# Another order of the 24 matmuls of a weight panel, in three stages of a one-core decoder layer

## The reference

```python
xn = _rmsnorm(h, norm1_g[l])
proj = xn @ w_in[l]                 # q, k, v, conv inputs, gated-attention inputs, three gate groups
ya = fox_attention(...) @ w_a_o[l]
yb = (sc_b * _causal_dwconv(sc_c * sc_h, conv_w[l])) @ w_b_o[l]
yc = (jax.nn.silu(rc) * oc) @ w_c_o[l]
mix = sigmoid(g_a + ..) * ya + sigmoid(g_b + ..) * yb + sigmoid(g_c + ..) * yc
h = h + mix @ w_o[l]
u = _causal_dwconv(_rmsnorm(h, norm2_g[l]) @ w_up[l], mlp_conv_w[l])
u_gate, u_up = jnp.split(u, 2, axis=-1)
h = h + (jax.nn.silu(u_gate) * u_up) @ w_down[l]
return _rmsnorm(h, final_norm_g)[:, N_META:]
```

## Time and profile before

| | |
|---|---|
| time of three runs | 1746.2, 1746.72 and 1748.32 us, median 1746.72 us |
| span of the profiled execution, first to last instruction | 1745.1 us |
| TensorE matmul busy | 1734.3 us (99%), 13429 instructions |
| TensorE weight loads busy | 1680.7 us (96%), 13429 instructions |
| VectorE, ScalarE, GpSimd busy | 1117.8, 763.7, 263.3 us |
| DMA | 320.62 MB, mean 184 GB/s |
| mean granted TensorE clock | 0.999 of 2.4 GHz |

### The profile page before, as it was taken

How to read it: one execution, slowest core, us unless ns; L and a number is a source line. 1 busy time by engine, 2 the same in 40 slices (tenths; PEclk the granted TensorE clock), 3 DMA queues, 4 the chain that set the end, 5 groups by cost and what they waited for, 6 DMA issues and landing times.

```text
span 1745.1 us, 34098 instructions
## 1 busy us (share of the span) xinstructions
PE 1734.3 (99%) x13429; PEld 1680.7 (96%) x13429; DVE 1117.8 (64%) x1607; ACT 763.7 (44%) x921; POOL 263.3 (15%) x494
## 2 busy tenths in 40 slices
PE   9999999999999999999999999999999999999998
PEld 8999999999999999999999999999999999888886
DVE  6857766667565554555556687777777777554454
ACT  6635444354354444444444444334444444343433
POOL 3153332630530000000000043321000000000000
PEclk9999999999999999999999999999999999999999
DMA  8567557666565655556645566666555565665654
GB/s 232 169 180 186 168 149 198 176 175 178 153 184 181 189 178 178 175 182 194 201 159 192 181 195 192 204 200 192 183 182 181 180 186 180 223 190 189 189 192 134
DMA packets 310296, 320.62 MB, mean 184 GB/s; under 512 B 17353, under 2 KB 285133, under 8 KB 310093
## 3 DMA queue, kind: packets, MB, share of 16 engines
q1 hardware_dynamic: 296861, 311.01, 58.2%
q0 software_dynamic: 12928, 7.80, 2.0%
q10 hardware_dynamic: 432, 0.79, 0.1%
HBM read 311.10 MB, written 2.11 MB: 179 GB/s over the span
## 4 chain that ended last, share of the span: by engine, by line
PE 99%; DVE 0%; DMA 0%; ACT 0%; SPq 0%; issue 0%; ACTq 0%; DVEq 0%
PE ps L1435 27%; PE ps L1437 27%; PE ps L1436 27%; PE ps L1693 5%; PE ps L1692 5%; PE ps L1691 5%; PE ps L1526 0%; DMA xb<-in_x_dram 0%; PE ps L1540 0%; PE ps L1565 0%; PE ps L1555 0%; PE ps L1556 0%; PE ps L1584 0%; PE ps L1585 0%; DVE xl L941 0%; DVE lo L896 0%
## 5 line engine op out<-in xcount | busy, mean ns | idle before, releaser
L896 DVE TENSOR_TENSOR lo<-raw,hi 128x1024 fp32r<-128x1024 f32 x584 | 709.9, 1229 | 494.4 <-ACT hi L627 490.2
L1435 PE MATMUL ps<-xh,hi 128*128 128x260 f32 (+1 forms) x3328 | 945.8, 284 | 0.2 <-DVE xl L941 0.2
L1437 PE MATMUL ps<-xh,lo 128*128 128x260 f32 (+1 forms) x3328 | 941.7, 283 | 0.0
L1436 PE MATMUL ps<-xl,hi 128*128 128x260 f32 (+1 forms) x3328 | 936.5, 281 | 0.0
L627 ACT CAST hi<-raw 128x1024 fp32r<-128x1024 f32 x584 | 604.8, 1048 | 671.8 <-PE ps L1437 539.0
L1436 PEld LDWEIGHTS ps<-xl,hi 128*128 128x128 f32 x3328 | 626.6, 188 | 0.2
L1435 PEld LDWEIGHTS ps<-xh,hi 128*128 128x128 f32 x3328 | 625.2, 188 | 1.3 <-issue 0.4
L1437 PEld LDWEIGHTS ps<-xh,lo 128*128 128x128 f32 x3328 | 624.7, 188 | 0.0
L610 POOL DMA_DIRECT2D hT<-h2b x128 | 69.6, 553 | 604.3 <-DVE h2b L1289 599.7
L1693 PE MATMUL ps<-lo,act_h 128*128 128x512 f32 x350 | 138.5, 396 | 0.0
L1692 PE MATMUL ps<-hi,act_l 128*128 128x512 f32 x350 | 137.3, 392 | 0.0
(11 more groups left out here) (298 smaller groups left out, 1383.6 us busy)
## 6 DMA issues: line engine op xcount, KB each, us to landing
raw<-in_w_in_dram SPq DMA_DIRECT2D x224, 512.0 KB, 3.6
raw<-in_w_up_dram SPq DMA_DIRECT2D x176, 512.0 KB, 4.6
raw<-in_w_down_dram SPq DMA_DIRECT2D x88, 512.0 KB, 4.7
raw<-in_w_o_dram SPq DMA_DIRECT2D x32, 512.0 KB, 3.4
raw<-in_w_in_dram SPq DMA_DIRECT2D x32, 256.0 KB, 4.2
raw<-in_w_a_o_dram SPq DMA_DIRECT2D x16, 512.0 KB, 4.3
raw<-in_w_b_o_dram SPq DMA_DIRECT2D x16, 512.0 KB, 3.3
raw<-in_w_c_o_dram SPq DMA_DIRECT2D x16, 512.0 KB, 3.3
```

Source lines behind the costliest of these rows:

```text
L896: nc.vector.tensor_tensor(part(ph, i, q, lo_all), raw[:, s, :], part(ph, i, q, hi_all).bitcast(F32), ALU.subtract).then_inc(lo_ready, 1)
L1435: nc.tensor.matmul(acc, w_hi, mh, start=first and j == 0, stop=False)
L1436: nc.tensor.matmul(acc, w_hi, ml, start=False, stop=False)
L1437: ins = nc.tensor.matmul(acc, w_lo, mh, start=False, stop=last and j == KJ - 1)
```

## The change

`use_ordered` takes the place of `use_panel` in the stages `GT`, `WO` and `UP`. It issues the same 24 matmuls with the same operands into the same two PSUM banks, in an order given by a list of (m, j, product). The order belongs to the panel's place in its trip. `BR` and `DN` are as before. The waits ahead of the panel and the increment of `panel_used` on the last matmul are as before; the start flag stands on the first matmul of each bank in the new order, the stop flag on the last.

```diff
+            KINDS = ((hi, 0), (hi, 1), (lo, 0))
+            HIGH, LOW_X, LOW_W = range(3)
+            def by_row(*rows):
+                return [(m, j, kind) for m in range(2) for j in rows for kind in range(3)]
+            def by_kind(*rows):
+                return [(m, j, kind) for m in range(2) for kind in range(3) for j in rows]
+            def by_two(*rows):
+                passes = (((0, HIGH), (0, LOW_W)), ((0, LOW_X), (1, LOW_X)), ((1, HIGH), (1, LOW_W)))
+                return [(m, j, kind) for both in passes for j in rows for m, kind in both]
+            def by_six(*rows):
+                return [(m, j, kind) for j in rows for m in range(2) for kind in range(3)]
+            UP_ORDERS = [by_row(0, 2, 1, 3)] * 4 + [by_row(0, 3, 1, 2)] * 4
+            GT_ORDERS = [by_kind(0, 1, 2, 3)] * 4 + [by_kind(0, 2, 1, 3)] * 4 + [by_kind(0, 2, 3, 1)] * 4
+            BO_ORDERS = [by_kind(0, 3, 2, 1)] * 6
+            WO_ORDERS = [by_six(0, 1, 2, 3)] * 4 + [by_two(0, 3, 1, 2)] * 4
+            def use_ordered(ph, i, q, st, moving, n, first, last, order):
+                pe.wait_ge(lo_ready, ph.panel(i, q) + 1)
+                s = ph.slot(q)
+                for at, (m, j, kind) in enumerate(order):
+                    weights, side = KINDS[kind]
+                    own = [k for k in range(len(order)) if order[k][0] == m]
+                    ins = nc.tensor.matmul(pset(st, n)[:, m, :], tiles(weights, s, j, m), moving(j)[side],
+                                           start=first and at == own[0], stop=last and at == own[-1])
+                ins.then_inc(panel_used, 1)
...
-                    use_panel(GT, i, q, st, mv, NC, kq == 0, kq == last)
+                    use_ordered(GT, i, q, st, mv, NC, kq == 0, kq == last, (GT_ORDERS + BO_ORDERS)[q])
...
-                    use_panel(WO, i, q, st, (lambda k0: lambda j: (mix_h[:, k0 + j, C0:T], mix_l[:, k0 + j, C0:T]))(kq * KJ),
-                              NC, kq == 0, kq == 3)
+                    use_ordered(WO, i, q, st, (lambda k0: lambda j: (mix_h[:, k0 + j, C0:T], mix_l[:, k0 + j, C0:T]))(kq * KJ),
+                                NC, kq == 0, kq == 3, WO_ORDERS[q])
...
-                    use_panel(UP, i, q, st, x_window(kq * KJ, C0, NC), NC, kq == 0, kq == 3)
+                    use_ordered(UP, i, q, st, x_window(kq * KJ, C0, NC), NC, kq == 0, kq == 3, UP_ORDERS[q])
```

## The result

The changed kernel takes 1750.15 us (median of 16 runs, 1749.17 to 1751.55) against 1746.71 us (16 runs). The ratio is 1.0019, 95% interval [1.0012, 1.0026]: slower by 3.4 us, small but clear of noise, where 1742.1 us was forecast. The time lies in the stated range, on the wrong side of no change.

A forecast was written before the change was run, and what follows sets the result against it. TensorE's matmul pace, 118.9 ns, was taken as the only bound. Changed panels at 2.84 instead of 2.853 us save 0.013 x 352 = 4.6 us: span 1740.5, plus 1.6 for the median, 1742.1 us; range 1731 to 1752 us.

The forecast's parts named there:

- A switch of the PSUM bank costs nothing: WO panels: alternating banks more often adds nothing, since the one switch seen costs nothing; at 0.01 us each, 2.6 us.
- The down projection is not touched: DN, which the change leaves as before: its window stays unchanged to 0.3 us.
- this interval: Bounds for the pace of the 352 changed panels: from 19 us less to 9.3 or 11 us more.
- the panel of 2.80 us: Nearer lower bound, from UP's timeline: every row group at 0.35 us instead of a 2.853 us panel, 19 us less.
- The sum: All 352 changed panels at 2 x 1.42 = 2.84 us instead of 2.853: 4.6 us less, giving 1742.1 us.
- the part that "moves least per matmul": UP, 176 panels, half of the work: only row-group order changes, rows still in threes, 8 of 24 followers change.
- GT: that a fresh moving operand at each matmul loses nothing: GT, 144 panels: moving operand and weights tile change every matmul; loading the same tile twice before brought no saving.
- The rival "slower": Changed panels lock into starts 120.0 ns apart; all of GT, WO and UP: 9.3 us more, 1756.0 us; chance 0.20.
- the half panel behind the 272-column ones: BR: first half of a 260-column panel following 272-column panels takes 1.44 us, 120.0 ns a matmul.
- The rival's point of decision: GT and part of WO: whether changing the moving row every matmul keeps the 120.0 ns rhythm instead of letting it die out.
- its figure for GT alone: Only GT in the 120.0 ns rhythm, 3456 matmuls x 1.1 ns: 1750.5 us.
- The rival "nothing": The changed kernel's time stays within 0.2%, about 3.5 us, of no change; chance 0.27.

The follow-up runs named there:

- 0213 in single products: Changed kernel with row groups in order 0, 2, 1, 3, one product at a time, in all 352 changed panels: 1758.6 us, ratio 1.0071.
- The survey: Up projection unrolled, each of 44 four-panel groups given its own sequence or window, some leaving the computation; the 24 row orders took 2.840 to 2.900 us a panel.
- single steps: Row groups 0, 1, 2, 3 in turn, one product at a time; changed kernel with this in all 352 changed panels: 1742.18 us, ratio 0.9974.
- double steps: Moves by two row groups; in the unrolled up projection, moving rows stepping by two over fixed weights took 2.920 us a panel.
- 01233210: Row groups visited in that sequence, one product per row, in four panels of the unrolled up projection: 2.920 us a panel.
- the survey of addresses: Up projection unrolled with moving windows and weights at chosen places and widths, plus ten down-projection orders; four starts 64 bytes apart took 2.840 us a panel, 128 bytes 2.920.
- one start: Unrolled up projection with the moving window at one place for every matmul: 2.880 us a panel at columns 8, 4 and 0, 2.911 at 10.

## Why the prediction was wrong

The forecast held in these steps. TensorE is the only bound and no wait came in. The pace is what changes, in GT, WO and UP alone. It depends on what runs before a matmul (0213 in single products took 2.86, 2.88 and 2.92 us). A switch of the PSUM bank costs nothing (2.854 and 2.840 us with a switch at every matmul, against 2.853 and 2.840). The down projection is not touched (244.08 and 244.09 us from its first matmul to its last).

**The step that failed** is "The present pace lies near the upper end of this interval. That is the main argument for a direction: there is more room below than above." The lower end of that interval was the panel of 2.80 us, and further down I had put the 112 ns of the 128-column float32 matmuls, by my estimate the time of a weight load. No run shows that it is the load's time, and no order tried reached either figure; the 2.80 us was in part a rounding, since it took row groups at 0.35 us from starts rounded to 0.01 us, and the shortest of the eight row groups of an UP panel takes 352.5 ns on the mean of the kernel before, or 2.82 us a panel. The survey puts the paces of 24 orders between 2.840 and 2.900 us, and one list reached 2.920. The old one, 2.853, is the fifth best or equal to it. Below it there was 0.013 us, above it 0.067. I had measured the room to bounds that none of these orders comes near, and not to what comparable orders take. The mechanism, a pace that depends on what came before, was right; the room and with it the direction were wrong.

**The sum** took "the pace of the quicker half panel for the whole panel", 2.84 us. That pace exists, 118.3 ns a matmul, and it is what the single steps reach; with all 352 panels there the time was 1742.18 us against the 1742.1 written down. But the halves of one panel are not two rhythms to choose from: 1.42 and 1.43 us are parts of one rhythm that repeats every 24 matmuls. Whether a given list reaches 2.84 could not be read from the trace of before, and I applied it to all eight lists. Two do, in 66 of the 352 panels.

**Part by part.** UP I called the part that "moves least per matmul": its first half lost 0.27 us in all, its second 0.02 us a panel and 1.66 us in all, about half of the loss. GT: that a fresh moving operand at each matmul loses nothing was right for 0123 and nearly so for 0321, and wrong for the other two lists. **The rival "slower"** came closest: it named a lock into a slower rhythm, and GT's second and third groups run at exactly 120.0 ns. That this is the rhythm of the half panel behind the 272-column ones is not shown; in unrounded starts that half takes 1.437 us, 119.8 ns a matmul, and the half after it is back at 1.432. The rival's point of decision was wrong. A change of moving row at every matmul doesn't keep the slow rhythm going, since single steps have it too and take 118.3 ns; which sequences do is not fully explained (double steps often, 01233210 without any). That its figure for GT alone, 1750.5 us, lies 0.35 us from the measured time is luck: GT lost 1.1 us and not 3.8, and WO and UP, which that figure leaves out, lost the rest. Had it been priced for two thirds of GT's gate panels, it would have come out at 64 x 24 x 1.1 ns = 1.7 us, close to what those 64 panels cost. **The rival "nothing"**, that the order has no effect, has the size: the ratio of 1.0019 lies within its 0.2%. But the order has an effect, from 2.840 to 2.920 us a panel in the lists tried. Two results of the survey of addresses show that the moving operand alone doesn't set the pace either: half the weight columns take 0.08 us off a panel in double steps, and weight tiles moved by 32 bytes add 0.04 us in single steps. With the tiles in place, a half or a quarter of the load changes nothing in the sequence 0123 (2.840 and 2.841 us against 2.840).

## What to carry to other kernels

In this kernel, where TensorE streams the rounded parts and the remainders without a gap, the order of independent matmuls was worth up to 2.8% of their time (2.84 against 2.92 us a panel). For 260 columns from column 12 the best list found cycles through four row groups in one direction, one product at a time, with starts 64 bytes apart modulo 256. It kept 2.84 us in all of the 352 panels but five, at the start and beside small float32 matmuls. Lists that go back and forth by the same step took 2.88 and 2.92 us, and from columns 8, 4 and 0 the same list took 2.880 us, no better than one start, and with 384 columns it was worse (4.280 against 4.240), so measure it where it is to run. Such a test fits into one unrolled loop, four panels for each candidate, since settled panels repeated to the nanosecond (2.840, 2.840 and 2.840 us). Give a candidate more than one predecessor: the same list, 0213 in single products, ran at 2.86, 2.88 or 2.92 us behind another list or a break in the stream. Measure the room by what comparable orders reach, not by the pace of another form of matmul (112 ns here, where no list of 260 columns went below 118.3).

## What the runs showed of the hardware

In this stream the pace was a rhythm into which a sequence locked. Settled panels of most lists repeated to 1 ns, and most of their mean distances between starts, 118.33, 119.17, 120.0, 120.83 and 121.67 ns, lie 0.833 ns apart, or 20 ns a panel (2.840, 2.860, 2.880, 2.900 and 2.920 us); others lie between (118.6, 118.89, 119.7, 121.3 ns). One start of 260 columns repeated gave 120.0 ns, from column 10 121.3 ns. One list, 0213 in single products, ran at 119.2, 120.0 or 121.7 ns a matmul by what preceded it: another list, or small float32 matmuls that broke the stream. In the sequences tried, the loss above 118.3 ns went away wholly or for the most part with half the weight columns (double steps from 121.7 to 118.3 ns, one start from 120.0 to 118.9), and weights read 32 bytes further on brought 120.0 ns where 118.3 had been. With a load of 32 columns the stream still took 118.4 ns for 260 columns; one start with 248 columns took 113.3; at 240, 192 and 128 columns, with 128 weight columns loaded each time, it was 111.7 ns. What sets this last figure is not shown: no run has fewer weight columns at these widths. Why no list of 260 columns went below 118.3 ns, why four starts 1024 bytes apart aren't as one start, and by what rule a sequence such as 01233210 locks into its pace, stays open.
